# A hybrid decoder layer on one core: the key norms are summed inside the projection, the low-rank products alternate row halves, and the chunk data are stored tile by tile

## The reference, cut to what matters

```python
us = u_r + mu_shift * (prev - u_r)                      # token shift
r, k, v, zw, za, zg = split(us)
w_raw = -softplus(-(w0 + tanh(zw) @ w_decay_up)) - 0.5  # low-rank, 64 rows
decay = exp(-exp(w_raw))
a = sigmoid(a0 + za @ w_a_up)                           # low-rank, 64 rows
g = sigmoid(zg) @ w_g_up                                # low-rank, 128 rows
kk = k * k_k
kk = kk / maximum(sqrt(sum(kk * kk, -1)), 1e-12)        # per head of 64
k = k * (1 + (a - 1) * k_a)
y, wkv = wkv_scan(r, decay, k, v, kk, a, wkv0)          # 10 chunks of 104 rows
out = (group_norm(y) + sum(r * k * r_k, -1) * v) * g    # bonus, then gate
```

## Time and profile before

| | |
|---|---|
| three runs | 2335.84, 2339.23, 2343.53 us (median 2339.23) |
| profiled execution | 2342.12 us, its span 2340.3 us |
| mean granted TensorE clock | 0.973 |
| TensorE, VectorE, ScalarE, GpSimd busy | 93%, 38%, 24%, 8% of the span |
| projection of the RWKV tiles ends | 218.7 us |
| forget logits end | 233.0 us |
| first low-rank product | 239.0 us |
| first matmul of the chunk loop | 315.05 us |

### The profile page before, as it was taken

How to read it: one execution, slowest core, us unless ns; L and a number is a source line. 1 busy time by engine, 2 the same in 40 slices (tenths; PEclk the granted TensorE clock), 3 DMA queues, 4 the chain that set the end, 5 groups by cost and what they waited for, 6 DMA issues and landing times.

```text
span 2340.3 us, 41764 instructions
## 1 busy us (share of the span) xinstructions
PE 2165.9 (93%) x16998; PEld 1771.0 (76%) x16998; DVE 879.0 (38%) x1405; ACT 554.0 (24%) x913; POOL 191.8 (8%) x186
## 2 busy tenths in 40 slices
PE   2999689999999999998889999969999999999995
PEld 1998357777777777655556566649999999999995
DVE  5333543433334434331777222153222222322334
ACT  3211522222222222211545220022102212201210
POOL 0000012122222222000211000000000000000000
PEclk9999789999999999999999999989999999999998
DMA  2112551110111221484556243111111111111111
GB/s 115 46 45 77 147 167 49 40 45 24 46 44 59 68 67 45 117 138 163 200 176 210 102 145 146 36 36 45 45 45 45 45 45 45 45 45 45 45 45 74
DMA packets 108443, 185.18 MB, mean 79 GB/s; under 512 B 65070, under 2 KB 65390, under 8 KB 104966
## 3 DMA queue, kind: packets, MB, share of 16 engines
q1 hardware_dynamic: 106022, 174.95, 23.5%
q10 hardware_dynamic: 2304, 8.50, 1.7%
HBM read 147.71 MB, written 35.71 MB: 78 GB/s over the span
## 4 chain that ended last, share of the span: by engine, by line
PE 85%; DVE 8%; DMA 3%; ACT 2%; SPq 1%; issue 1%; DVEq 0%; ACTq 0%
PE ps L279 38%; PE ps L345 18%; PE ps L255 10%; PE ps L867 4%; PE ps L868 3%; PE ps L1181 1%; DVE arena L1637 1%; DVE normed L327 1%; PE ps L1165 1%; PE ps L809 1%; DVE arena L1786 1%; PE ps L1047 1%; PE ps L984 1%; PE ps L1106 1%; DMA weights<-in_wu 1%
## 5 line engine op out<-in xcount | busy, mean ns | idle before, releaser
L345 PE MATMUL ps<-normed,weights 128*128 128x350 f32 x1344 | 449.6, 477 | 8.9 <-ACTq L1303 5.8
L279 PE MATMUL ps<-h_split,w_split 128*128 128x350 f32 x2304 | 373.9, 324 | 16.6 <-DVE h_split L1937 16.6
L279 PEld LDWEIGHTS ps<-h_split,w_split 128*128 128x128 f32 x2304 | 371.8, 190 | 19.0 <-issue 12.9
L279 PE MATMUL ps<-ff_split,w_split 128*128 128x350 f32 x2304 | 371.4, 323 | 0.0
L279 PEld LDWEIGHTS ps<-ff_split,w_split 128*128 128x128 f32 x2304 | 370.9, 189 | 0.0
L345 PEld LDWEIGHTS ps<-normed,weights 128*128 128x128 f32 x1344 | 245.0, 193 | 131.7 <-issue 20.6
L867 PEld LDWEIGHTS ps<-arena 64*64 64x64 f32 x2400 | 148.6, 135 | 46.1 <-issue 26.5
L1924 DVE TENSOR_TENSOR arena<-arena,ps 128x1050 f32 (+1 forms) x40 | 50.0, 1249 | 353.3 <-PE ps L279 266.2
L255 PE MATMUL ps<-fox,weights 128*128 128x350 f32 x576 | 173.0, 461 | 3.0 <-DVE fox L1914 3.0
L1997 POOL TENSOR_TENSOR arena<-arena,constants 64x512 f32<-64x512 f32 x120 | 132.5, 1104 | 487.6 <-DVE arena L1637 420.8
L867 PE MATMUL ps<-arena 64*64 64x64 f32 x2400 | 163.7, 220 | 1.0
(11 more groups left out here) (260 smaller groups left out, 2187.2 us busy)
## 6 DMA issues: line engine op xcount, KB each, us to landing
weights<-in_wu SPq DMA_DIRECT2D x122, 512.0 KB, 3.3
normed<-in_vp SPq DMA_DIRECT2D x64, 260.0 KB, 4.6
normed<-in_kp SPq DMA_DIRECT2D x64, 256.0 KB, 5.1
arena<-chunk_dram SPq DMA_DIRECT2D x10, 1248.0 KB, 5.5
arena<-gate_dram SPq DMA_DIRECT2D x16, 525.0 KB, 5.1
chunk_dram<-arena SPq DMA_DIRECT2D x12, 520.0 KB, 6.8
chunk_dram<-fox SPq DMA_DIRECT2D x12, 520.0 KB, 4.2
arena<-samp_dram SPq DMA_DIRECT2D x10, 512.0 KB, 9.4
```

The source lines that it names most:

```text
L279: last = pe.matmul(PS[:, 3 * s + g, 0:G], ws[:, s, wh, k * P:(k + 1) * P], x[xh][:, k, g * G:(g + 1) * G], start=(k == 0 and wh + xh == 0) ...
L345: last = self.pe.matmul(PS[:, 6 + m % 2, 0:G], W[:, s, k * P:(k + 1) * P], HT[:, k, g * G:(g + 1) * G], start=(k == 0), stop=(k == KT - 1))
```

## The change: what it does

1. Sums of squared keys. ScalarE squares the scaled keys in one pass with `Square` into `YT`, before it copies unit 11 out. TensorE sums them with 12 matmuls of 350 columns that stand in the last four steps of units 11, 12 and 13, in banks 6 and 7. VectorE clips each group as it comes. ScalarE takes all four logarithms and then all four exponentials between the copies of units 13 and 14. KK is then one instruction for each p.
2. The low-rank products alternate the row halves (group, then half), the gate products follow in the same loop, and the sums for the bonus come behind the whole loop, with two PSUM slots in turn.
3. `chunk_dram` is laid out by tile, so a store has one run of 4160 B for each partition instead of ten of 416 B, and a chunk's load has 24 runs of 416 B instead of one of 9984 B. r and v are stored during the projection. The gate stays in SBUF and GpSimd reads it there; the bonus alone goes through `bg_dram`.

```diff
         PS = ctx.enter_context(nc.psum_tensor("ps", [P, 8, 512], F32))
-        chunk_dram = nc.dram_tensor("chunk_dram", [P, NC, 6, HP, C], F32, kind="Internal").ap()
-        bg_dram = nc.dram_tensor("bg_dram", [P, 2 * HP, TT], F32, kind="Internal").ap()
+        chunk_dram = nc.dram_tensor("chunk_dram", [P, 6, HP, TP], F32, kind="Internal").ap()
...
+            def keep_tile(kind, p, src):
+                sp.dma_start(chunk_dram[:, kind, p, :], src[:, p, 0:TP]).then_inc(prep_stored, 16)
+
+            load_pairs(1, PV_RW - 2)
+            sp.wait_ge(mixed, HP)
+            for p in range(HP):
+                keep_tile(0, p, RW[:, 0:HP])
+            load_pairs(PV_RW - 2, PV_RW)
+            sp.wait_ge(mixed, 3 * HP)
+            for p in range(HP):
+                keep_tile(2, p, RW[:, 2 * HP:3 * HP])
...
             for p in range(HP):
                 sp.wait_ge(lora_read, 2 * p + 1)
                 keep_tile(3, p, LW)
-            for p in range(HP):
+                sp.wait_ge(kk_made, p + 1)
+                keep_tile(4, p, KK)
                 sp.wait_ge(krk_made, p + 1)
                 keep_tile(1, p, RW[:, HP:2 * HP])
-                sp.wait_ge(kn_made, p + 1)
-                keep_tile(4, p, KK)
+                sp.wait_ge(bb_made, p + 1)
                 keep_tile(5, p, BB)
+            for p in range(HP):
                 sp.wait_ge(bon_made, p + 1)
-                keep_bg(p)
-                sp.wait_ge(gt_read, NG * (p + 1))
-                keep_bg(HP + p)
+                sp.dma_start(bg_dram[:, p, :], BON[:, p, :]).then_inc(bg_stored, 16)

             def load_chunk(c):
-                src = chunk_dram[:, c] if isinstance(c, int) else chunk_dram[:, bass.ds(c, 1)]\
-                    .rearrange("p o a b t -> p (o a) b t")
-                sp.dma_start(CH, src).then_inc(st_in, 16)
+                here = slice(c * C, (c + 1) * C) if isinstance(c, int) else bass.ds(c * C, C)
+                sp.dma_start(CH, chunk_dram[:, :, :, here]).then_inc(st_in, 16)
...
+            def key_sums(n0):
+                def ready(k):
+                    if k >= 4:
+                        n = n0 + k - 4
+                        p, g = divmod(n, NG)
+                        pe.wait_ge(ksq_made, p + 1)
+                        if n >= 2:
+                            pe.wait_ge(ksq_read, n - 1)
+                        pe.matmul(PS[:, 6 + n % 2, 0:G], blk, YT[:, p, g * G:(g + 1) * G], start=True, stop=True)\
+                          .then_inc(ksq_done, 1)
+                return ready
+
+            pe_unit_split(pe, PV_RW - 2, 0, H0, key_sums(0), of=RWKV)
+            pe_unit_split(pe, PV_RW - 2, 1, H0, key_sums(4), of=RWKV)
+            pe_unit_split(pe, PV_RW - 1, 0, H0, key_sums(8), of=RWKV)
...
+            pe.wait_ge(ksq_read, NG * HP)
             for p in range(HP):
-                for m in range(2):
-                    if p:
-                        pe.wait_ge(lora_read, 2 * p - 1 + m)
-                    rows = slice(m * HD, (m + 1) * HD)
-                    for g in range(NG):
+                if p:
+                    pe.wait_ge(lora_read, 2 * p)
+                for g in range(NG):
+                    for m in range(2):
+                        rows = slice(m * HD, (m + 1) * HD)
                         last = pe.matmul(PS[:, 3 * m + g, 0:G], wl[rows, p * P:(p + 1) * P],
                                          RW[rows, 12, g * G:(g + 1) * G], start=True, stop=True)
-                    last.then_inc(lora_done, 1)
-
...
                 for g in range(NG):
                     n = NG * p + g
                     if n >= 2:
                         pe.wait_ge(gt_read, n - 1)
                     pe.matmul(PS[:, 6 + n % 2, 0:G], wg[:, p * P:(p + 1) * P], RW[:, 13, g * G:(g + 1) * G],
                               start=True, stop=True).then_inc(gt_done, 1)
...
+            pe.wait_ge(lora_read, 2 * HP)
+            for p in range(HP):
                 pe.wait_ge(krk_made, p + 1)
-                if p:
-                    pe.wait_ge(bon_made, p)
-                summed(1, prk[p % 2], krk_done)
-
-            pe.wait_ge(ksq_read, HP)
+                if p >= 2:
+                    pe.wait_ge(bon_made, p - 1)
+                for g in range(NG):
+                    last = pe.matmul(PS[:, 3 * (p % 2) + g, 0:G], blk, prk[p % 2][:, g * G:(g + 1) * G], start=True,
+                                     stop=True)
+                last.then_inc(krk_done, 1)
+
...
+            act.wait_ge(mixed, 2 * HP)
+            for p in range(HP):
+                act.activation(YT[:, p, :], RW[:, HP + p, :], ACT.Square, scale=par[:, V_KK + p:V_KK + p + 1])\
+                   .then_inc(ksq_made, 1)
             for s in range(2):
-                keep(PV_RW - 1, s, RW[:, 2 * PV_RW - 2 + s, :])
+                keep(PV_RW - 2, s, RW[:, 2 * PV_RW - 4 + s, :])
+                act_split(act, PV_RW - 1, s, of=RWKV)
+            keep(PV_RW - 1, 0, RW[:, 2 * PV_RW - 2, :])
+            for p in range(HP):
+                act.wait_ge(ksq_read, NG * (p + 1))
+                order(act.activation(YT[:, p, :], YT[:, p, :], ACT.Ln))
+            for p in range(HP):
+                act.activation(YT[:, p, :], YT[:, p, :], ACT.Exp, scale=-0.5).then_inc(kinv_made, 1)
+            keep(PV_RW - 1, 1, RW[:, 2 * PV_RW - 1, :])
...
+            def key_sums(n0):
+                for n in range(n0, n0 + 4):
+                    p, g = divmod(n, NG)
+                    dve.wait_ge(ksq_done, n + 1)
+                    dve.tensor_scalar(YT[:, p, g * G:(g + 1) * G], PS[:, 6 + n % 2, 0:G], 1e-24, None, ALU.max)\
+                       .then_inc(ksq_read, 1)
...
+            key_sums(0)
+            mix_pair(PV_RW - 2, True, (0,))
+            key_sums(4)
+            mix_pair(PV_RW - 2, True, (1,))
+            key_sums(8)
             mix_pair(PV_RW - 1, False)
...
+            for p in range(HP):
+                dve.wait_ge(kinv_made, p + 1)
+                dve.scalar_tensor_tensor(KK[:, p], RW[:, HP + p, :], par[:, V_KK + p:V_KK + p + 1], YT[:, p, :],
+                                         ALU.mult, ALU.mult).then_inc(kk_made, 1)
+            dve.wait_ge(kk_made, HP)
+
+            def bonus(p):
+                dve.wait_ge(krk_done, p + 1)
+                dve.tensor_tensor(g3(BON[:, p]), grp(p % 2), g3(RW[:, 2 * HP + p, :]), ALU.mult).then_inc(bon_made, 1)
+
+            for p in range(HP):
                 r_, k_ = RW[:, p, :], RW[:, HP + p, :]
-                order(dve.tensor_scalar(KK[:, p], k_, par[:, V_KK + p:V_KK + p + 1], None, ALU.mult))
-                dve.tensor_tensor(ptmp[p % 3], KK[:, p], KK[:, p], ALU.mult).then_inc(ksq_made, 1)
                 dve.wait_ge(lora_read, 2 * p + 2)
-                order(dve.tensor_scalar(mtmp, BB[:, p], 1.0, par[:, V_KA + p:V_KA + p + 1],
-                                        ALU.subtract, ALU.mult))
+                order(dve.tensor_scalar(mtmp, BB[:, p], 1.0, par[:, V_KA + p:V_KA + p + 1], ALU.subtract, ALU.mult))
                 order(dve.scalar_tensor_tensor(k_, mtmp, 1.0, k_, ALU.add, ALU.mult))
                 if p >= 2:
                     dve.wait_ge(krk_done, p - 1)
                 dve.scalar_tensor_tensor(prk[p % 2], r_, par[:, V_RK + p:V_RK + p + 1], k_, ALU.mult, ALU.mult)\
                    .then_inc(krk_made, 1)
...
+                dve.tensor_tensor(BB[:, p], KK[:, p], BB[:, p], ALU.mult).then_inc(bb_made, 1)
+                if p >= 1:
+                    bonus(p - 1)
+            bonus(HP - 1)
...
-                ch_pool.done(pool.tensor_tensor(here, here, BGc[:, HP:2 * HP], ALU.mult), "gate")
+                ch_pool.done(pool.tensor_tensor(here, here, GT[:, :, bass.ds(c * C, C)], ALU.mult), "gate")
```

More of the change, by code:

```diff
@@ L471, in build @@
         r_rw = Region(rw_end, ar_end - rw_end)
-        BG = r_rw.take(2 * HP, TT)
-        BON, GT = BG[:, 0:HP], BG[:, HP:2 * HP]
-        sh_in = r_rw.take(RW_T, DEC)
-        sh_out = r_rw.take(RW_T, DEC + 1)
-        mtmp = r_rw.take(TT)
-        ptmp = [YT[:, 0, :], YT[:, 1, :], r_rw.take(TT)]
-        prk = [YT[:, 2, :], YT[:, 3, :]]
+        BON = r_rw.take(HP, TT)
+        prk = [YT[:, 0, :], YT[:, 1, :]]
+        r_top = Region(ar_end - RW_T * (2 * DEC + 1) - TT, RW_T * (2 * DEC + 1) + TT)
+        GT_at = r_top.at - HP * TT
+        GT = view(GT_at, HP, TT)
+        assert r_rw.at <= GT_at
+        sh_in = r_top.take(RW_T, DEC)
+        sh_out = r_top.take(RW_T, DEC + 1)
+        mtmp = r_top.take(TT)
         d_col_ready = sem("d_col_ready")
@@ L505, in build @@
         gst = r_c2.take(4, NH)
-        BGc = r_ch.take(2 * HP, C)
+        BGc = r_ch.take(HP, C)
+        assert r_ch.at <= GT_at
         bonus_added = sem("bonus_added")
@@ L649, in _ @@
             sp.wait_ge(prep_stored, 16 * 6 * HP)
-            sp.wait_ge(bg_stored, 16 * 2 * HP)
+            sp.wait_ge(bg_stored, 16 * HP)
             sp.wait_ge(sh_stored, 16)
@@ L796, in _ @@
             pe.wait_ge(f_read, 1)
```

(39 more changed lines are left out.)

54 lines of the change are left out of this document (12 added, 42 removed).

## The result

The changed kernel takes 2311.94 us (median of 4 runs, 2308.75 to 2313.93), the kernel before, on the same chip, 2337.53 (4 runs, 2335.47 to 2343.53). The ratio is 0.9885, with a 95% interval from 0.9861 to 0.9909: faster by 25.6 us. Repeated, it took 2311.01 us (median of 6 runs), and the ratio was 0.9896 (0.9878 to 0.9915). The forecast was 2319, with its own range from 2315 to 2323: right in sign and place, but 7 us too slow.

A forecast was written before the change was run, and what follows sets the result against it. TensorE holds 85% of the chain, so only the 76.1 us preparation can gain: chunk loop at 244.8 + 49.4 + 0.5 = 294.7 instead of 315.05, 20.3 us won, 2321.8 profiled, 2319 as median, range 2315 to 2323.

The forecast's parts named there:

- Key sums, +7.1: Projection: twelve fp32 matmuls summing squared keys lengthen TensorE's chain by 7.1 us, ends 7.0 and 9.
- To the first product, -1.3: From forget logits to first low-rank product: one table load of 1.28 us goes, so 1.3 us less than 6.04.
- Low-rank loop: Preparation: alternated products, 5.4 us a tile at full clock, 7.7 at half; last sigmoid read 23.5 us after the first product.
- The ring: Repeating turn per tile: two sigmoids, gate copy, third gate product, next tile's six products; 5.4 us at full clock.
- The new wait: Bonus: its sums stand behind the whole loop, so VectorE idles over 8 us; last bonus at 40.8 to 42.0.
- Stores set the end: End of preparation: ten tiles at 333 GB/s, 1.6 us each, last landing 49.4 us after the first low-rank product.
- a sign of being wrong: End of preparation: a bonus landing right behind VectorE would contradict the forecast, which had the last store some 7 us later.
- First chunk load, +0.5: Start of chunk loop: the first load in 416 B pieces lands in 6.6 us, costing 0.5 us, ends 0 and 3.
- compute as the end: End of preparation: stores at 396 GB/s or an earlier clock let compute set the end, 2316 to 2313 us; chance 19%.
- The slow low-rank loop: Low-rank loop: half clock throughout, or row halves not side by side; near +8 us, 2327; chance 19%.
- The rival on pieces: First chunk load: 416 B runs move at half rate, 8.4 us instead of 4.2, giving 2323 us; chance 5%.
- The slower case: Projection: stores of r and v delay weights, TensorE stalls in units 11 to 13, 25 us lost, 2344; chance 0.05.

## Why the prediction had the place right and the gain too small

1. **Key sums, +7.1.** Measured 8.0 (226.67 - 218.71). The sums that ran without a wait cost 0.59 in the chain, as priced; one waited 0.46 for VectorE's read of the first, as I had said the third might, and four were 0.12 to 0.24 longer. It happened in one unit of three.
2. **To the first product, -1.3.** Right: 18.9 us from the start of the logits to the first product, forecast 19.0.
3. **Low-rank loop.** The ring is 5.41 us at full clock, forecast 5.4. The half clock held for the first round's products (3.89 us), not for one and a half rounds: the last sigmoid is read 22.3 us after the first product, not 23.5.
4. **The new wait.** VectorE idles 9.27 us, forecast over 8. The first sums come at 25.3 (forecast 26.7), and the last bonus ends 40.4 us after the first product, just below the 40.8 to 42.0 given.
5. **Stores set the end: this step failed, in its rate.** It gave 49.4 us from the first product to the last landing; measured were 44.9 (290.4 - 245.5). The mis-sized term is the rate: I took 333 GB/s, 1.6 us a tile, between 264, measured for pieces of 416 B, and 396, measured for long rows. The new stores have long rows and moved 378 to 407 GB/s, 1.3 us a tile. The ten tiles took (44.9 - 29.9 - 3.7) / 9 = 1.26 us each from the measured first issue, 29.9 (forecast 31.3). So 3.1 of the 4.5 us are the rate and 1.4 the earlier first issue. The row that answered to the changed stores was the long one, and I halved the distance instead of asking which row has the form of the new transfer.

   At this rate the stores and VectorE nearly tie. Stores back to back give 29.9 + 3.7 + 9 x 1.32 = 45.5, VectorE's last bonus and its own transfer 40.4 + 4.4 = 44.8. Between 281 and 282 us the queue ran short (DMA share 0.73) and waited for VectorE's fourth tile, so there were no ten stores without a gap. Behind that it was full again, for SyncE issues the bonuses last. The last tile landed one transfer behind the last bonus, not 7 us behind it, which the prediction had named as a sign of being wrong. With the old layout, at 227 GB/s, the stores do set the end, 5.9 us later. Issuing the first bonuses earlier was not tried; the queue's share at the end, some 0.9 us, is about what it could win.
6. **First chunk load, +0.5.** Nothing on the chain. It landed in 7.2 us instead of 6.6, but TensorE's first 32 instructions of the chunk loop are the projection of the other branch and need no chunk; the first step that does came 11.57 us after the loop's start, before 12.19.

Added up: 294.7 + 0.9 (step 1) - 4.5 (step 5, and in it 3 and 4) - 0.5 (step 6) = 290.6, where 290.52 was measured. Of the 7.1 us between the forecast and the median these steps are 4.2, less 1.0 for the chunks. Another 1.7 are that the kernel before itself now has a median of 2337.5 and not the 2339.2 from which I counted. The last 2.2 lie within the interval and have no cause that a run shows.

Of the rivals, compute as the end comes nearest to what happened: it gave 2316 to 2313, with stores at 396 GB/s as its condition. The slow low-rank loop did not come: the clock rose after the first round, and the halves ran side by side. The rival on pieces has this for it: in pieces of 416 B stores moved 227 GB/s against 378 to 407, and chunk loads of that form took 7.1 us against 5.6 to 6.2. The Trainium skill ("DMA: Bandwidth & Descriptors", Specifications) asks for at least 512 B a transfer for line rate. The trace agrees for stores, while loads took 1.15 to 1.3 times as long, not the double that the rival took. As a price on the end it was nothing, since no engine waited for that load. The slower case is refuted by the one wait of 0.46 us in the projection and by storing r and v late.

Left open: the 0.11 us a chunk. The layout is excluded from both sides (64.88 us with the old one in the changed kernel, 64.77 with the new one in the kernel before). So are the bonus load of half the size and the gate read from SBUF: all four kernels with the bonuses last have both, and their chunks are 64.77 us apart. The time goes in one place, VectorE's pause ahead of its first mask; the first line is the changed kernel, the second the one with the bonuses last:

```profile
369.92 3.32 DVE L1656 TENSOR_TENSOR arena<-ps,constants 104x832 f32<-104x832 f32 x3 [0.24 <-DVE arena L1651]
361.87 3.32 DVE L1653 TENSOR_TENSOR arena<-ps,constants 104x832 f32<-104x832 f32 x3
```

In the first VectorE starts 0.24 us after the end of the instruction before, in the second 0.13 us. The code of the chunk loop is the same in both; only the preparation ahead of it differs. What lengthens the pause no run shows.

## What to carry to other kernels

When a long ring of waits goes, list for each engine its whole work in the freed stretch before choosing what is late next: here VectorE's order (a bonus that blocks the next tile) was the bound at 290.5 us, TensorE's gates and sums at 282.6, and TensorE's sums with ScalarE's last copies behind them at 280.1. A wait for a result that nothing else needs soon (the bonus) belongs behind the work that others wait for; that was worth 8.2 us, for two more buffers. Price a transfer by the row with its own piece length, not by the mean of short and long ones.

## What the runs showed of the hardware

- Stores in rows of 4 KB a partition moved 378 to 407 GB/s, in pieces of 416 B 227 GB/s with the DMA engines fully busy (share 1.08). SyncE's own issue of three such stores grew from 1.8 to 5.6 us, so short pieces hold back the issuing engine too.
- Six fp32 products of 64 rows, alternating between the row halves, took 2.04 us. Not alternated but behind one wait they took 2.73, and with each half behind its own sigmoid 3.06, so in those orders too the halves ran partly side by side.
- After 4.62 us of idling TensorE was granted 1.2 GHz in all eleven kernels that have this wait. How long it then worked before it had 2.4 GHz again varied: 4.5 us in the changed kernel (granted clock 0.50 in 249.5 to 250, 0.99 in 250 to 251) and 4.3 to 6.2 us in the seven with alternated products. In the six with the halves apart it was 4.3 to 9.7 us, and the order does not decide it: two kernels with the same products in the same order had 8.7 and 4.8 us, the kernel before and its copy with the new layout 9.5 and 4.3. TensorE was busy throughout in the kernel with 9.7 us:

```profile
250.00:255.00 5.00, 5.00 (x13) 3.01 (x12) 2.85 (x3) 2.19 (x3) 0.00 (x0) 0.50 0.53 213
```
